# Transposing the modulation rows in 32x32 blocks on VectorE, and putting them into columns by four matmuls per layer

## The chip, the cores and the metric

The kernel runs on one core of a Trainium2 chip. The metric is the device time of one execution in microseconds (us). A core has five engines that run side by side, each through its own list of instructions in order, and they meet only at semaphores: TensorE (PE; its weight loads are listed apart as PEld), VectorE (DVE), ScalarE (ACT), GpSimd (POOL) and SyncE (SP), which here issues the weight transfers. TensorE reads SBUF and writes PSUM, which has eight banks of 128 x 512 fp32.

## The reference, cut to what matters

Two transformer-like blocks follow each other on 256 tokens of width 1024. The first has two layers (attention, cross attention to a memory, a gated feed-forward with a convolution of width 3 over tokens); the second has two layers whose inputs are modulated:

```python
def conv_glu(x, w_in, conv_w, conv_b, w_out):          # feed-forward, layers 0 and 1 of block one
    gate, val = jnp.split(x @ w_in, 2, axis=-1)        # (256, 1024) @ (1024, 5632)
    gate = depthwise conv of width 3 over tokens (gate) + conv_b
    return (jax.nn.gelu(gate, approximate=False) * val) @ w_out

def ada_params(sc, w, b):                              # block two; sc (n, D), w (D, 6 D)
    mod = sc @ w + b
    return [t[:, None, :] for t in jnp.split(mod, 6, axis=-1)]
```

`sc` is silu of the conditioning vector, once for the context and once for the latent tokens, so `sc @ w` is a product of 2 rows with a 1024 x 6144 matrix, for each of the two layers of block two.

## The kernel before, in words

Large matrices come in slabs of 1 MB (128 partitions x 2048 fp32). SP transfers them one after the other into a ring of four slots; a slot is refilled when PE has begun far enough ahead (`slab_begun`). Large products run in three passes for precision: ScalarE rounds a slab to `w_hi` (two instructions of 128x1024, L2497, function `hi`), GpSimd subtracts it from the slab to get `w_lo` (two of 128x1024, L1990, function `lo`), and PE adds `w_hi x_hi + w_lo x_hi + w_hi x_lo` (L1510 to L1514). PE may start a slab only when both halves of its `w_lo` are there (`lo_ready`).

The change sits in the two feed-forwards of block one, stages `f0` and `f1` (function `network` of each engine). There are 22 units of work, 20 in a loop of five rounds of four (`L.rounds(5, ...)`), two behind it. Between their slabs lie the 24 slabs of `ada_w`: block two's modulation of layer 0 is computed during `f0`, that of layer 1 during `f1`, since those matmuls need the slab only in its plain fp32 form. For unit n the engines do, each in this order:

- PE: `ada` (L1719): 8 matmuls of the modulation slab n, four of them side by side in the four groups of 32 partitions (quadrants) of bank 5 or 6, in turn; so the sum over the contraction is spread over the four quadrants, each with the 2 rows that are wanted. Then `col_T_split`: 48 matmuls of the weights of unit n into bank n mod 4. Then `ada_T` (L1736): two matmuls with the copied rows `modR` as the stationary operand and `pick` as the moving one (L1744). `pick` has two columns with ones where a partition is row 0 or 1 of its quadrant; so each adds the four quadrants and turns the two rows into two columns of bank 4. `ada_T` comes behind the copy `ada_out` of the same unit.
- ACT (L2542 to L2592): `ada_out`, a copy of bank 5 or 6 to `modR` (128x256, L2548, by way of L2435); the copy of bank n mod 4 to `raw` (128x512, also L2435); `hi` of unit n+2; a wait for `pre_ready` from DVE; the gelu (L2574).
- DVE (`gated`, L2145): waits for `raw`; the convolution (L2155, L2157, L2159; the last announces `pre_ready`); waits for the gelu; product with `val` (L2164); split into `h_hi` and `h_lo` (L2165, L2166).
- POOL: `lo` of unit n+2, two instructions, each waiting for its half from ACT.

Behind the 22 units PE does the last two modulation slabs (22 and 23) and their `ada_T`; then comes stage `fo0` or `fo1` (`rows_split`, L1549), 11 slabs with 24 matmuls each (L1564), each slab again behind `hi` and `lo`. DVE adds the bias to the 96 columns of bank 4 (`modulation`, L380, L384) behind its 22 units. In layer 1 more hangs on that: DVE goes on with `gains` and the variance of the context rows (L483, L528), POOL computes the power for it (`rstd(second=True)`) ahead of `lo` of slab 3 of `fo1` (L2060), and PE transposes the context rows ahead of slab 4 (`turn_ctx`, L1703).

Of the kernel before, what the change touches and what calls it, by code (L numbers as in the profile page):

```python
# [30 lines left out]
P = 128  # L31
# [78 lines left out]
for _name, _n in [("lambda", 256), ("subln", 128), ("dt_bias", 64), ("a_log", 64), ("d_skip", 32)]:  # L110
# [7 lines left out]
             "sq_ready", "wdt_hi", "wdt_ready", "c_split", "pre0_ready", "dt_ready", "yz_ready",  # L118
             "y_hi", "o_hi", "var_o", "rstd_o", "x_hi", "res_ready"]

# [55 lines left out]
def build(nc, slabs, x_in, xT_in, memT_in, ctx_in, pt_in, row_in, ln_in, wdt_in, out):  # L176
    with ExitStack() as ctx:
# [66 lines left out]
        half16 = small[:, 136:152]  # L244
        pick = small[:, 152:154]
        modA = small[:, 168:184]
# [34 lines left out]

        modR = cut(15360, 4, 256)
        raw = cut(11264, 4, 512)
# [1144 lines left out]
        def _(pe):  # L1428
# [3 lines left out]
            def free_of(b):  # L1432

                return free[last.get(b, "act")][b]
# [312 lines left out]

            def network(layer):
# [5 lines left out]
                for_rounds("act")  # L1754
                marks[stage] = {q: L.now(("act", q)) for q in range(8)}
                turned = turned_x()
                pe.wait_ge(free_of(4), frees(4))
                for b_ in (5, 6):
                    pe.wait_ge(free_of(b_), frees(b_))
                    last[b_] = "act"  # L1760
                per = {("act", q): 2 if q > 4 else 1 for q in (0, 1, 2, 3, 5, 6)}
                with L.rounds(5, per | {("took", "lo_ready"): 8}) as i:
                    for u in range(4):

                        ada(stage, 2 * u, u, 2 * i)
                        col_T_split(stage, 2 * u + 1, u, waits=turned if u == 0 else None)
                        ada_T(i * 4 + u, u)
                for u in range(2):
                    ada(stage, 2 * u, u, 10)
                    col_T_split(stage, 2 * u + 41, u)  # L1770
                    ada_T(20 + u, u)
# [297 lines left out]
        def _(v):  # L2069
# [75 lines left out]
            def gated(i, u, conv):  # L2145
# [78 lines left out]
            def network(stage, conv=None):  # L2224
# [6 lines left out]
                if conv is not None:  # L2231
                    one |= {("own", "v_step"): 4, ("own", "pre_ready"): 1}
                per = {k: 4 * n for k, n in one.items()} | {("raw", b): 1 for b in range(4)}
                with L.rounds(5, per) as i:
                    for u in range(4):
                        gated(i, u, conv)
                for u in range(2):
                    gated(5, u, conv)

            split_x("dq", by_chunks)  # L2240
# [23 lines left out]
            for tt in range(NT):  # L2264
# [7 lines left out]
                for g in (1, 2):  # L2272
# [18 lines left out]
            v.wait_ge(S["consts"], L.took("consts"))  # L2291
            v.tensor_reduce(pick, ident.rearrange("p (q c) -> p c q", q=4)[:, 0:2, :], AX.X,
                            ALU.add).then_inc(S["pick_ready"], 1)
# [135 lines left out]
        def _(a):  # L2429
# [112 lines left out]
            def network(func, conv, layer):  # L2542

                net, out_ = (f"f{layer}", f"fo{layer}") if conv else (f"h{layer}", f"ho{layer}")

                def ada_out(u):

                    copy_out(5 + u % 2, modR[:, u, :], bank[5 + u % 2][:, 0:256])  # L2548

# [9 lines left out]
                def one(i, u):  # L2559
                    if conv:  # L2560
                        ada_out(u)
                    else:
# [13 lines left out]
                if conv:  # L2576
                    per |= {("took", "pre_ready"): 4} | {(k, b): 2 for k in ("bank", "freed") for b in (5, 6)}
                if conv:
                    hi(net, 3)
                with L.rounds(5, per) as i:  # L2580
# [4 lines left out]
                if conv:  # L2585
                    for u in (2, 3):
                        ada_out(u)
                for j in range(1 if conv else 2, 11):
# [196 lines left out]
```

## Time and profile before

| | us |
|---|---|
| time, median of 3 runs (lowest to highest) | 2195.94 (2191.88 to 2202.35) |
| time of the profiled execution | 2195.72 |
| its span, first to last instruction | 2194.0 |
| PE busy | 2012.7 (92%) |
| POOL busy | 1255.3 (57%) |
| DVE busy | 1163.3 (53%) |
| ACT busy | 983.6 (45%) |
| stage f0 with the modulation of layer 0 | 306.1 to 484.6 |
| stage f1 with the modulation of layer 1 | 960.9 to 1141.2 |

A profile row names the line of the kernel, the engine, the operation, what it writes and reads with shapes, and its time. Brackets behind a row of a timeline give the idle time of the engine just before it and what ended that. Most buffers of the network are cut from one tensor, so `raw`, `pre`, `act` and `modR` all read `arena` in the rows. An fp32 matmul shows as two records (x192 for 96 instructions).

### The profile page before, as it was taken

What the parts mean: (1) busy time and instruction counts of PE and PEld (TensorE: products, weight loads), DVE (VectorE), ACT (ScalarE), POOL (GpSimd) and SP (SyncE); (2) the same over time, 40 slices, a digit from 0 to 9 for tenths busy, and PEclk for the clock granted to TensorE, in tenths of its full rate; (3) what the DMA queues carried; (4) which work ended last, traced back from release to release, by engine and by line L of the source; (5) the groups of instructions that cost most, each with busy time, mean ns of one, the idle gap of its engine ahead of it and who ended that gap; (6) DMA issues with size and microseconds to landing.
All of it is one profiled execution on the core that took longest, in us unless ns stands there. A gap on an engine that the chain in (4) does not pass through costs nothing.

```text
span 2194.0 us, 34395 instructions
## 1 busy us (share of the span) xinstructions
PE 2012.7 (92%) x13901; PEld 1792.8 (82%) x13901; DVE 1163.3 (53%) x1567; ACT 983.6 (45%) x1545; POOL 1255.3 (57%) x579
## 2 busy tenths in 40 slices
PE   7879999999899979979999899899999997978997
PEld 7768888878899966868888778788779986947996
DVE  8783247771200083157775655678846852745641
ACT  4454444543344373434453454444436645424542
POOL 8647566668688604546669334200087895415885
PEclk9989999999899999999999999999999998988999
DMA  6324366665455404366764222211144553313553
GB/s 246 132 97 175 114 245 266 270 234 181 167 191 191 175 1 154 116 235 254 276 247 176 73 77 94 80 58 58 39 154 154 191 191 116 135 58 137 186 185 115
DMA packets 48320, 342.30 MB, mean 156 GB/s; under 512 B 5264, under 2 KB 6288, under 8 KB 7248
## 3 DMA queue, kind: packets, MB, share of 16 engines
q1 hardware_dynamic: 45968, 328.22, 41.0%
q0 software_dynamic: 2240, 12.49, 1.5%
q8 instruction: 81, 1.33, 0.2%
q14 instruction: 31, 0.25, 0.0%
HBM read 339.65 MB, written 1.05 MB: 155 GB/s over the span
## 4 chain that ended last, share of the span: by engine, by line
PE 67%; DVE 20%; ACT 4%; DMA 3%; issue 3%; POOL 2%; DVEq 0%; SPq 0%; ACTq 0%; POOLq 0%
PE bank L1564 12%; PE bank L1510 9%; PE bank L1514 9%; PE bank L1512 9%; DMA ring<-slabs_dram 3%; PE bank L1484 3%; DVE arena L811 2%; PE bank L1608 2%; PE bank L1146 2%; PE bank L1149 2%; PE bank L1148 2%; PE bank L1545 2%; PE bank L1544 2%; PE bank L1542 2%; PE bank L1316 2%
## 5 line engine op out<-in xcount | busy, mean ns | idle before, releaser
L1990 POOL TENSOR_TENSOR w_lo<-ring,w_hi 128x1024 fp32r<-128x1024 f32 x360 | 877.6, 2463 | 333.2 <-ACT w_hi L2497 333.0
L1510 PE MATMUL bank<-x_hi,w_hi 128*128 128x256 f32 x2176 | 620.5, 285 | 27.8 <-POOL w_lo L1990 16.3
L1514 PE MATMUL bank<-x_lo,w_hi 128*128 128x256 f32 x2176 | 622.8, 286 | 0.0
L2497 ACT ACTIVATE w_hi<-ring 128x1024 fp32r<-128x1024 f32 x448 | 448.6, 1052 | 279.4 <-DMA ring<-slabs_dram 279.2
L1510 PEld LDWEIGHTS bank<-x_hi,w_hi 128*128 128x128 f32 x2176 | 419.2, 193 | 48.8 <-issue 44.7
L1514 PEld LDWEIGHTS bank<-x_lo,w_hi 128*128 128x128 f32 x2176 | 418.0, 192 | 0.0
L1512 PE MATMUL bank<-x_hi,w_lo 128*128 128x256 f32 x1472 | 414.2, 281 | 0.0
L2435 ACT ACTIVATE arena<-bank 128x512 f32<-128x512 f32 (+1 forms) x274 | 146.3, 548 | 349.4 <-PE bank L1514 242.1
L1990 POOL TENSOR_TENSOR w_hi<-ring,w_hi 128x1024 fp32r<-128x1024 f32 x88 | 217.7, 2496 | 130.8 <-ACT w_hi L2497 130.8
L1512 PEld LDWEIGHTS bank<-x_hi,w_lo 128*128 128x128 f32 x1472 | 282.5, 192 | 0.0
L1512 PE MATMUL bank<-x_hi,w_hi 128*128 128x256 f32 x704 | 201.5, 286 | 0.0
L2164 DVE TENSOR_TENSOR arena<-arena 128x256 f32<-128x256 f32 x88 | 112.7, 1281 | 110.0 <-ACT arena L2574 107.2
L403 POOL TENSOR_TENSOR w_lo<-ring,w_swo 128x1024 fp32r<-128x1024 f32 x16 | 39.9, 2526 | 185.0 <-ACT w_swo L911 185.0
L394 POOL TENSOR_TENSOR w_lo<-ring,w_half 128x1024 fp32r<-128x1024 f32 x32 | 76.9, 2409 | 113.8 <-ACT w_half L902 113.8
L1512 PEld LDWEIGHTS bank<-x_hi,w_hi 128*128 128x128 f32 x704 | 136.6, 194 | 0.0
L2395 DVE CUSTOM_DVE_ANT_0 arena<-bank,dist 128x512 f32<-128x512 f32 x32 | 22.1, 692 | 213.2 <-PE bank L1882 212.6
L2166 DVE TENSOR_TENSOR h_lo<-arena,h_hi 128x256 f32 (+1 forms) x88 | 118.5, 1347 | 10.1
L634 DVE SCALAR_TENSOR_TENSOR arena<-bank,pt,arena 128x508 f32<-128x508 f32 (+3 forms) x128 | 87.3, 682 | 62.6 <-ACT arena L917 59.0
L1564 PE MATMUL bank<-w_hi,h_hi 128*128 128x512 f32 x352 | 112.9, 398 | 2.1 <-issue 1.6
L1564 PE MATMUL bank<-w_lo,h_hi 128*128 128x512 f32 x352 | 112.8, 398 | 0.0
L1564 PE MATMUL bank<-w_hi,h_lo 128*128 128x512 f32 x352 | 112.5, 397 | 0.0
L1146 PE MATMUL bank<-s_hi,w_half 128*128 128x512 f32 (+1 forms) x288 | 103.9, 361 | 1.9 <-DVE s_lo L572 1.9
(323 smaller groups left out, 3808.2 us busy)
## 6 DMA issues: line engine op xcount, KB each, us to landing
ring<-slabs_dram SPq DMA_DIRECT2D x312, 1024.0 KB, 4.8
lnrow<-ln_dram POOLq DMA_DIRECT2D x6, 1024.0 KB, 5.1
xt<-xT_dram SPq DMA_DIRECT2D x1, 1024.0 KB, 5.7
xt<-memT_dram POOLq DMA_DIRECT2D x1, 1024.0 KB, 13.3
x<-x_dram POOLq DMA_DIRECT2D x1, 1024.0 KB, 17.2
arena<-ctx_dram POOLq DMA_DIRECT2D x1, 1024.0 KB, 8.2
lnrow<-ln_dram POOLq DMA_DIRECT2D x2, 512.0 KB, 4.0
res<-x POOLq DMA_DIRECT2D x2, 512.0 KB, 2.9
```

Of the source, the lines that this page charges most:

```text
L394: pool.tensor_tensor(half_slab(w_lo, c), half_slab(ring, c), half_of(c)[:, :, :].bitcast(F32), ALU.subtract).then_inc(S["lo_ready"], 1)
L634: ins = v.scalar_tensor_tensor(out=d3[:, :, lo:hi], in0=s3[:, :, lo + o:hi + o], scalar=pt[:, scw + k * 32 + j:scw + k * 32 + j + 1], in1= ...
L1146: ins = pe.matmul(dst, wh[:, k, :], hi_(k), start=(k == 0), stop=False)
L1510: ins = pe.matmul(dst, wh[:, k, c], src[0][:, k, :], start=(k == 0), stop=False)
L1512: ins = pe.matmul(dst, wl[:, k, c], src[0][:, k, :], start=False, stop=False)
L1514: ins = pe.matmul(dst, wh[:, k, c], src[1][:, k, :], start=False, stop=(k == KC - 1))
L1564: ins = pe.matmul(bank[2 * tt + h][:, :], st, w[:, k, h * 512:(h + 1) * 512], start=(first and n == 0), stop=(end and n == 2))
L1990: pool.tensor_tensor(dst[:, c], ring[:, s, c], w_hi[:, s, c].bitcast(F32), ALU.subtract).then_inc(S["lo_ready"], 1)
L2164: step(v.tensor_tensor(act[:, u, :], act[:, u, :], val, ALU.mult))
L2166: v.tensor_tensor(h_lo[:, j, :], act[:, u, :], h_hi[:, j, :].bitcast(F32), ALU.subtract).then_inc(S["hT_ready"], 1)
L2435: a.activation(dst, bank[b][:, :] if src is None else src, ACT.Copy if not kw else ACT.Identity, **kw).then_inc(free["act"][b], 1)
L2497: a.activation(w_hi[:, g % RING, c], ring[:, g % RING, c], ACT.Copy) \
```

## The change

`modR` is no longer copied by ScalarE and turned by PE for each slab. VectorE reads bank 5 or 6 and transposes it in 32x32 blocks into `modR` (two buffers now, `turn_ada`), as the first thing of each unit; ScalarE then copies 16 of the 256 columns (two of each block of 32) to a buffer `modC` that keeps all 24 slabs (`ada_out`). `ada_T` goes. In its place `ada_columns` runs once per layer, ahead of slab 2 of `fo0` and `fo1`: four matmuls, one for each quadrant, with `pick` (now 32 columns) as the stationary operand. Bank 4 has the same 96 columns in the end.

```diff
@@ tensor engine @@
-                fill(ins, b, "act")
-
-            def ada_T(j, r):
-                pe.wait_ge(free_of(5 + r % 2), frees(5 + r % 2))
-                for ch in range(2):
-                    at = 2 * (2 * j + ch)
-                    dst = bank[4][:, at:at + 2] if isinstance(j, int) \
-                        else bank[4][:, 0:96][:, bass.ds(at, 2)]
-                    ins = pe.matmul(dst, modR[:, r, ch * P:(ch + 1) * P], pick, start=True,
-                                    stop=True)
-                return ins
+                fill(ins, b, "dve")
+
+            def ada_columns(layer):
+                pe.wait_ge(free_of(4), frees(4))
+                pe.wait_ge(S["ada_kept"], 24 * (layer + 1))
+                kept = modC.rearrange("p u (c q s) -> p q (u c) s", c=2, q=4)
+                for q in range(4):
+                    ins = pe.matmul(bank[4][32 * q:32 * (q + 1), 0:96].rearrange("p (a s) -> p a s", s=2),
+                                    pick, kept[:, q, :, :], start=True, stop=True)
+                fill(ins, 4, "dve")
...
                         col_T_split(stage, 2 * u + 1, u, waits=turned if u == 0 else None)
-                        ada_T(i * 4 + u, u)
...
-                ada_T(22, 2)
-                fill(ada_T(23, 3), 4, "dve")
-                rows_split(f"fo{layer}", hook=turn_ctx if layer else None)
+                def between(j):
+                    if j == 2:
+                        ada_columns(layer)
+                    if layer:
+                        turn_ctx(j)
+                rows_split(f"fo{layer}", hook=between)
@@ vector engine @@
+            def turn_ada(u):
+                b = 5 + u % 2
+                v.wait_ge(full["dve"][b], L.filled(b))
+                v.transpose(modR[:, u % 2, :], bank[b][:, 0:256]).then_inc(free["dve"][b], 1)
+                v.wait_ge(free["dve"][b], L.freed(b))
...
                     for u in range(4):
+                        if conv is not None:
+                            turn_ada(u)
                         gated(i, u, conv)
                 for u in range(2):
+                    if conv is not None:
+                        turn_ada(u)
                     gated(5, u, conv)
+                if conv is not None:
+                    turn_ada(2)
+                    turn_ada(3)
@@ scalar engine @@
-                def ada_out(u):
-                    copy_out(5 + u % 2, modR[:, u, :], bank[5 + u % 2][:, 0:256])
+                def ada_out(u, j):
+                    b = 5 + u % 2
+                    a.wait_ge(free["dve"][b], L.up(("turned", b)))
+                    a.activation(modC[:, j, :].rearrange("p (c s) -> p c s", s=2),
+                                 modR[:, u % 2, :].rearrange("p (c s) -> p c s", s=32)[:, :, 0:2],
+                                 ACT.Copy).then_inc(S["ada_kept"], 1)
```

## Rows read from the trace of the kernel before

**Rows 1.** Stretch f0: busy PE, PEld, DVE, ACT, POOL; clock, DMA share, GB/s.

```profile
306.10:484.60 178.50, 167.01 (x1537) 151.04 (x1537) 129.06 (x130) 86.11 (x124) 109.32 (x45) 0.98 0.70 271
```

**Rows 2.** Timeline of PE in f0: an unhindered step, then a stalled one.

```profile
391.97 0.50 PE L1744 MATMUL bank<-small,arena 128*128 128x2 f32 x4
392.40 1.07 PE L1730 MATMUL bank<-ring,sc_in 128*32 128x256 f32 x16
...
415.64 0.60 PE L1744 MATMUL bank<-small,arena 128*128 128x2 f32 x4 [1.93 <-ACT arena L2435]
```

**Rows 3.** Waits: PE's before L1744, both layers; DVE's for raw in f0.

```profile
  ACT arena L2435: 21.1, 13
...
DVE arena L2155 <- ACT arena L2435: 27.5, 4, 21.4
```

**Rows 4.** Timelines of DVE, ACT and POOL, 346.8 to 356.1: unit 4 of f0.

```profile
347.70 0.41 DVE L2155 TENSOR_SCALAR arena<-arena,pt 128x256 f32<-128x256 f32 x1 [1.39 <-ACT arena L2435]
...
348.89 2.40 DVE L2159 SCALAR_TENSOR_TENSOR arena<-arena,pt 128x255 f32<-128x255 f32 x1
351.84 1.98 DVE L2164 TENSOR_TENSOR arena<-arena 128x256 f32<-128x256 f32 x1 [0.56 <-ACT arena L2574]
...
354.38 0.42 DVE L2166 TENSOR_TENSOR h_lo<-arena,h_hi 128x256 f32 x1
...
346.84 0.60 ACT L2435 ACTIVATE arena<-bank 128x512 f32<-128x512 f32 x1 [1.90 <-PE bank L1514]
347.33 2.00 ACT L2497 ACTIVATE w_hi<-ring 128x1024 fp32r<-128x1024 f32 x2
...
351.32 0.42 ACT L2574 ACTIVATE arena<-arena 128x256 f32<-128x256 f32 x1 [0.68 <-DVE arena L2159]
...
348.46 5.08 POOL L1990 TENSOR_TENSOR w_hi<-ring,w_hi 128x1024 fp32r<-128x1024 f32 x2 [3.41 <-ACT w_hi L2497]
```

**Rows 5.** Timeline of DVE, 399 to 410: a cast beside POOL; the loop's return.

```profile
405.44 2.26 DVE L2165 CAST h_hi<-arena 128x256 f32 x1
...
408.98 0.42 DVE L2155 TENSOR_SCALAR arena<-arena,pt 128x256 f32<-128x256 f32 x1 [0.73 <-DVE h_lo L2166]
```

**Rows 6.** DVE reading PSUM (a timeline row); ACT's small copy (groups by form).

```profile
870.10 2.87 DVE L2207 TENSOR_TENSOR x_lo<-bank,x_hi 128x512 fp32r<-128x512 f32 x4 [5.00 <-ACT x_hi L2468]
...
L2609 ACT ACTIVATE sc_in<-pt 128x16 f32<-128x16 f32 x1 | 0.2, 218 | 0.0
```

**Rows 7.** Timeline of DVE: the first product of f0 and of f1.

```profile
319.64 2.34 DVE L2164 TENSOR_TENSOR arena<-arena 128x256 f32<-128x256 f32 x1 [2.81 <-ACT arena L2574]
...
976.78 2.31 DVE L2164 TENSOR_TENSOR arena<-arena 128x256 f32<-128x256 f32 x1 [4.73 <-ACT arena L2574]
```

**Rows 8.** Timelines of DVE, ACT, POOL, PE at f0's end; last row: the chain.

```profile
474.17 0.42 DVE L2166 TENSOR_TENSOR h_lo<-arena,h_hi 128x256 fp32r<-128x256 f32 x1
...
482.73 1.94 DVE L2164 TENSOR_TENSOR arena<-arena 128x256 f32<-128x256 f32 x1 [0.55 <-ACT arena L2574]
...
489.63 0.26 DVE L384 TENSOR_TENSOR mod<-bank,pt 128x96 f32<-128x96 f32 x1
...
470.74 0.60 ACT L2435 ACTIVATE arena<-bank 128x512 f32<-128x512 f32 x1 [1.31 <-PE bank L1514]
...
477.93 0.60 ACT L2435 ACTIVATE arena<-bank 128x512 f32<-128x512 f32 x1 [4.38 <-PE bank L1514]
...
479.55 14.69 POOL L1990 TENSOR_TENSOR w_lo<-ring,w_hi 128x1024 fp32r<-128x1024 f32 x6 [11.76 <-ACT w_hi L2497]
...
482.96 1.67 PE L1744 MATMUL bank<-small,arena 128*128 128x2 f32 x8 [2.86 <-ACT arena L2435]
...
484.62 57.93 PE bank L1564 x239
```

**Rows 9.** Timelines at f1's end: ACT's last copy of raw, POOL's power.

```profile
1134.54 0.60 ACT L2435 ACTIVATE arena<-bank 128x512 f32<-128x512 f32 x1 [2.85 <-PE bank L1514]
...
1151.07 0.71 POOL L1967 TENSOR_TENSOR small<-small 128x2 f32<-128x2 f32 x1
```

More of the change, by code:

```diff
@@ L118 @@
              "sq_ready", "wdt_hi", "wdt_ready", "c_split", "pre0_ready", "dt_ready", "yz_ready",
-             "y_hi", "o_hi", "var_o", "rstd_o", "x_hi", "res_ready"]
+             "y_hi", "o_hi", "var_o", "rstd_o", "x_hi", "res_ready", "ada_kept"]
 class Ledger:
@@ L244, in build @@
         half16 = small[:, 136:152]
-        pick = small[:, 152:154]
+        pick = small[:, 264:296]
         modA = small[:, 168:184]
@@ L280, in build @@
         goT = tri[:, :, :, :].rearrange("p a b c -> p (a b c)").rearrange("p (a b) -> p a b", a=8)
-        modR = cut(15360, 4, 256)
+        modR = cut(15360, 2, 256)
+        modC = cut(15872, 24, 16)
         raw = cut(11264, 4, 512)
@@ L1755, in network @@
                 marks[stage] = {q: L.now(("act", q)) for q in range(8)}
+                marks[f"ada{layer}"] = {b: L.now(("dve", b)) for b in (5, 6)}
                 turned = turned_x()
-                pe.wait_ge(free_of(4), frees(4))
                 for b_ in (5, 6):
                     pe.wait_ge(free_of(b_), frees(b_))
-                    last[b_] = "act"
-                per = {("act", q): 2 if q > 4 else 1 for q in (0, 1, 2, 3, 5, 6)}
+                    last[b_] = "dve"
+                per = {("act", q): 1 for q in range(4)} | {("dve", q): 2 for q in (5, 6)}
                 with L.rounds(5, per | {("took", "lo_ready"): 8}) as i:
@@ L1770, in network @@
                     col_T_split(stage, 2 * u + 41, u)
-                    ada_T(20 + u, u)
                 ada(stage, 4, 2, 10)
                 ada(stage, 5, 3, 10, last_one=True)
-                ada_T(22, 2)
-                fill(ada_T(23, 3), 4, "dve")
-                rows_split(f"fo{layer}", hook=turn_ctx if layer else None)
+                def between(j):
[4 more added lines that the diff above has]
+                rows_split(f"fo{layer}", hook=between)
             pe.wait_ge(S["consts"], L.took("consts"))
@@ L2233, in network @@
                 per = {k: 4 * n for k, n in one.items()} | {("raw", b): 1 for b in range(4)}
+                if conv is not None:
+                    per |= {(k, b): 2 for k in ("bank", "freed") for b in (5, 6)}
                 with L.rounds(5, per) as i:
                     for u in range(4):
+                        if conv is not None:
+                            turn_ada(u)
                         gated(i, u, conv)
                 for u in range(2):
+                    if conv is not None:
+                        turn_ada(u)
                     gated(5, u, conv)
+                if conv is not None:
+                    turn_ada(2)
+                    turn_ada(3)
             split_x("dq", by_chunks)
@@ L2291, in _ @@
             v.wait_ge(S["consts"], L.took("consts"))
-            v.tensor_reduce(pick, ident.rearrange("p (q c) -> p c q", q=4)[:, 0:2, :], AX.X,
+            v.tensor_reduce(pick, ident.rearrange("p (q c) -> p c q", q=4), AX.X,
                             ALU.add).then_inc(S["pick_ready"], 1)
@@ L2560, in one @@
                     if conv:
-                        ada_out(u)
+                        ada_out(u, i * 4 + u)
                     else:
@@ L2576, in network @@
                 if conv:
-                    per |= {("took", "pre_ready"): 4} | {(k, b): 2 for k in ("bank", "freed") for b in (5, 6)}
+                    per |= {("took", "pre_ready"): 4, ("turned", 5): 2, ("turned", 6): 2}
                 if conv:
+                    L.n.update({("turned", b): marks[f"ada{layer}"][b] for b in (5, 6)})
                     hi(net, 3)
@@ L2586, in network @@
                     for u in (2, 3):
-                        ada_out(u)
+                        ada_out(u, 20 + u)
                 for j in range(1 if conv else 2, 11):
```

## The prediction

> **What bounds the kernel now.** PE is busy for 92% of the whole, so the first guess is that whatever leaves PE is won. I read the two stages that the change touches by themselves, and there it is not so. The busy time by stretch gives PE 167.0 of 178.5 us in f0, DVE 129.1, POOL 109.3, ACT 86.1 [rows 1]; nobody looks full but PE. Next the timeline of PE. An unhindered step has its last `ada_T` at 391.97 and the next `ada` at 392.40, so `ada_T` holds PE for 0.43 us of a step; a stalled one stood idle for 1.93 us before `ada_T`, for the copy on ACT [rows 2]. These stalls come to 21.1 us over both layers, in 13 places [rows 3]. A copy of 0.4 us doesn't make a PE wait for 1.9: ACT does it late, since in its list it stands behind the gelu of the unit before, and the gelu behind DVE's convolution. So DVE is asked next.
>
> Rows 4 show one unit on the three engines. The copy of `raw` ends at 347.44 (346.84 + 0.60), DVE starts 0.26 later, its third instruction (L2159) takes 2.40 us, the gelu ends at 351.74, the product takes 1.98, and DVE is done at 354.80. The same instructions take 0.48 and 0.43 us when POOL is still. POOL's two subtractions run from 348.46 to 353.54: L2159 ends 0.3 us behind POOL's first, L2164 0.3 behind its second. A cast beside POOL's work took 2.26 us in the same way [rows 5]. So DVE stands still for most of POOL's 5 us in each unit. DVE waited for `raw` in only four of f0's 22 units, and 21.4 of those 27.5 us are before the first [rows 3]: its 129 us of work [rows 1], with the gelu and the semaphores between, fill the stage. In f0 and f1 DVE and POOL set the pace together with PE, with nothing to spare. That is where the change puts more work.
>
> **The change part by part.** *Removed from PE:* 22 `ada_T` in the loop at 0.43 us and the waits before them. By itself that is 2 x 22 x 0.43 = 19 us and up to 21.1 us, if PE still sets the pace; it is idle time gained if not.
>
> *The order that is new.* Before, ACT could copy `raw` of unit n+1 as soon as PE had filled the bank and the gelu of unit n was done, while DVE was still busy with the product and the split of unit n. Now the copy of `raw` stands in ACT's list behind `ada_out`, which waits for `turn_ada` of the same unit, and that stands in DVE's list behind the split of unit n. Behind the waiting ACT instruction are queued: the copy of `raw`, `hi` for unit n+2 and so POOL's `lo` for it, and the gelu. So a closed ring arises: DVE's split, transpose, small copy, copy of `raw`, `hi`, POOL's two subtractions (which hold up DVE), DVE's product, split. I walk it once.
>
> - From the end of a `raw` copy to the end of the split: 354.80 - 347.44 = 7.36 us [rows 4]. This row is the right one since there `hi` followed the copy at once (347.33), as it will: the slab is asked for when PE begins unit n, and by then ACT is late.
> - The transpose. No row shows one. It reads 256 columns of PSUM. Of DVE instructions that read PSUM the one of 512 columns takes 2.87/4 = 0.72 us [rows 6] and the one of 96 columns 0.26 [rows 8]: 1.1 ns a column, so 0.43 us. Bounds: 0.26 (the smallest row) and 0.86 (twice the rate's price, should 4-byte blocks go at half speed); I take 0.43, and 0.14 us for the semaphore before it. Beside POOL it may stand or not: a cast from SBUF does (2.26), the PSUM row L384 was done in 0.26 us at 489.63, inside POOL's 479.55 to 494.24 [rows 8]. In this ring it comes 1.4 us behind POOL's end, so it is not hit.
> - ACT's copy of 16 columns: 0.22 us, the row of that size [rows 6], and 0.03 before it. Bounds 0.15 and 0.4.
> - The copy of `raw`, 0.60, less 0.1 that ACT overlaps (the next one started at 347.33, before 347.44): 0.5.
>
> Together 7.36 + 0.57 + 0.25 + 0.50 = 8.68 us a unit. At the loop's return DVE stands 0.73 us before its first instruction [rows 5], of which some 0.28 are there in any unit (0.26 in [rows 4]): 0.45 more in each fourth unit, now inside the ring.
>
> The Trainium skill has two prices for the transpose. VectorE: DVE Perf Modes, section on the TRN2 errata, gives a PSUM to SBUF instruction 120 cycles and one for each element at 0.96 GHz, an estimate of 0.39 us; its section on the three transpose paths has 0.311 us for 128x128 in bf16, to which 128 more columns at the trace's 1.1 ns would add up to 0.45. By the one the sum would be 2 us less, by the other 1 us more; no run here shows it yet.
>
> *f0.* The first unit is untouched up to the product, since DVE has nothing before it. That starts at 319.64 and takes 2.34 [rows 7]; cast and split end 1.0 later, at 322.96; then transpose, small copy and copy of `raw` (1.32): the `raw` copy of unit 1 ends at 324.3. Units 1 to 19 are followed by POOL's work of unit n+2 (`hi` runs up to unit 21): 324.3 + 18 x 8.68 + 4 x 0.45 = 482.3 for unit 19, 491.5 for unit 20 with the last return. Unit 20 has no POOL work beside it: in the rows its `raw` copy ended at 471.34 and its split at 474.59, so 3.25, and 1.2 for the new steps: `raw` of unit 21 is copied at 496.0. Before it was at 478.53 [rows 8]. PE is no limit: `lo` of unit 21 is ready 6.1 us behind `raw` of 19 (353.54 - 347.44), so at 488.4, its matmuls last about 5.8 (a step of 7.2 less `ada` and `ada_T`), so 494.2. The stage is late by 17.5 us.
>
> *The end of f0.* PE starts fo0 when POOL has `lo` of its slab 0: 484.62, 6.1 us behind the last `raw` [rows 8], before as after; the 2.86 us that PE waited in the last `ada_T` [rows 8] lay under this wait, so nothing is won. But ACT's `hi` of slab 1 now stands behind the small copies of slabs 22 and 23, and these behind DVE's two last transposes. DVE's product ends at 484.67 [rows 8], 6.1 behind `raw`; POOL is idle then, so cast, split and two transposes take 0.3 + 0.4 + 0.9, the last small copy 0.25: `hi` starts at 8.0, its first half takes 1.0, POOL 4.9 for its two (14.69/3): slab 1 is ready 13.9 to 14.0 us behind `raw`. PE is done with slab 0 at 6.1 + 5.3 (58/11) = 11.4. It waits 2.5 us. From then on POOL's 4.9 a slab is under PE's 5.3. The four matmuls, 8 records of 96 columns, are bounded by the 1.07 us of 16 records of 256 columns at L1730 [rows 2] from above and by 8/16 x 96/256 of it, 0.2, from below; I take 0.5 us a layer. In f0 the sum is 17.5 + 2.5 + 0.5 = 20.5 us.
>
> *f1.* The product of the first unit starts at 976.78, 2.31 [rows 7]: `raw` of unit 1 at 981.4, of unit 21 at 1153.1, against 1135.14 [rows 9]: 18.0 late. The same 2.5 and 0.5. Then one new wait: POOL's power (0.71 [rows 9]) stands ahead of `lo` of slab 3 and hangs on DVE's `modulation`, which now waits for `ada_columns` ahead of slab 2. From the matmuls' end: DVE's 0.26, two small instructions 0.4, power 0.71, slab 3's `lo` 4.9, with semaphores 6.4, while PE has slab 2's 5.3: 1.1 us of stall. Behind the waiting POOL are slabs 3 to 10, behind the waiting DVE the context rows, which PE wants only ahead of slab 4: 5 us to spare. Sum 18.0 + 2.5 + 0.5 + 1.1 = 22.1.
>
> **Sum.** 20.5 + 22.1 = 42.6 us on the profiled execution's 2195.72 (span 2194.0), which is within 0.3 us of the median 2195.94: 2238.3.
>
> **The rivals.**
>
> *Unchanged ring (same).* POOL's subtractions could shift so that the new steps lie under them: two of DVE's instructions are held for 2 us each, and if a transpose and a `raw` copy ran in those 4 us, the unit would stay at its present mean, 178.5/22 = 8.1 with all stalls. Then only the ends are lost, 3.0 + 4.1: 2203. Against it: POOL cannot start until ACT's `hi`, and that is behind the very copy. From none to all hidden the loop gives 0 to 36 us.
>
> *PE sets the pace (faster).* If the ring closes in less than 7.19 - 0.43 = 6.76 us, PE is the bound and gains 19 us of `ada_T` and its stalls, 21.1 less 2 x 2.9 that lay under POOL at the two ends [rows 8]: 2195.7 - 34 = 2161. For it: the 21.1 us are real and their cause goes. Against: DVE alone needs 7.3 in [rows 4]. It decides from a ring under 6.76.
>
> *A dear transpose (slower still).* At 0.86 us, 48 x 0.43 = 21 us more at most, of which 44 lie in the ring: 19, so 2257. It decides from the first microsecond, since nothing in the ring covers it.
>
> *The transposes alone (slower, smaller).* ACT's order doesn't bite, as where PE or the DMA is late anyway, and only DVE's 0.57 us a unit are added, 44 x 0.57 = 25; the places where DVE waited for `raw` behind the first unit, 6.1 us in f0 [rows 3] and taken twice, swallow 12, and the ends cost 7: 2195.7 + 25 - 12 + 7 = 2216. Against it: the copy order is in the lists, whoever else is late.
>
> **How the numbers follow.** The forecast, 2238.3 with 2227 to 2249 of its own, 0.50; dear transpose 0.13; transposes alone 0.17; unchanged 0.12; faster 0.08. The range reaches from 2211 to 2259: it leaves out the last two, 0.20 together. Half a per cent is 11 us, about what a measurement of this kernel can tell from no change: faster 0.08, same 0.12, slower 0.80.
>
> **What would show it.** In the profile after: a line `modR`'s transpose of about 0.43 us, 24 a layer; the `raw` copies on ACT released no longer by PE but following DVE; steps of 8.7 us and PE idle some 2 us before each unit's first matmul, released by POOL's `w_lo`; f0 about 196 us long and f1 about 198; a gap of 2.5 us behind the first 24 matmuls of fo0. It is wrong if the steps stay at 8.1 (the ring hides), if they fall to 6.8 (PE's pace), or if PE's waits are named for bank 5 or 6 instead of `w_lo`. The granted clock, 0.98 in f0 now [rows 1], should not matter, as PE has 2 us to spare in each step.

## The result, and the profile after

| | before | after |
|---|---|---|
| time, median (lowest to highest), us | 2197.62 (2191.88 to 2202.35) | 2245.36 (2240.49 to 2247.87) |
| profiled execution, us (span) | 2195.72 (2194.0) | 2240.49 (2238.8) |
| stage f0, us | 178.4 | 200.3 |
| fo0, to the first sum that DVE takes from it | 58.1 | 58.6 |
| stage f1, us | 180.4 | 203.2 |
| fo1, to the first sum that DVE takes from it | 58.9 | 62.7 |

The kernel is slower: the ratio is 1.0216, with a 95% interval of 1.0184 to 1.0247. The profiled executions differ by 44.8 us, of which the two stages have 21.9 and 22.8, fo0 0.5 and fo1 3.8; the rest of the kernel was 4.2 shorter, 3.4 of them ahead of f0, where only `pick` was made wider. That part isn't the change's: in the profiled runs below that have the same lists up to f0 as the kernel after, f0 begins anywhere from 301.4 to 306.4 us.

First the busy time of the engines over the whole, then of PE, PEld, DVE, ACT and POOL in f0 and f1 (the last three columns are the granted clock, the DMA share and GB/s).

```profile
PE 2003.7 (89%) x13725; PEld 1779.0 (79%) x13725; DVE 1181.7 (53%) x1615; ACT 974.0 (44%) x1545; POOL 1258.5 (56%) x579
...
302.70:503.00 200.30, 163.25 (x1441) 145.81 (x1441) 136.37 (x152) 79.51 (x120) 109.19 (x44) 0.94 0.62 241
979.33:1182.50 203.17, 165.22 (x1440) 147.08 (x1441) 135.28 (x153) 78.55 (x120) 109.50 (x44) 0.93 0.62 243
```

Against [rows 1], PE's work in f0 fell by 3.8 us and the stage grew by 21.9; every engine has more idle time than before. No engine is full, so I looked for a circle of waits. One unit shows it, on the timelines of DVE, ACT, POOL and PE of the kernel after (start, duration, engine, line; in brackets the idle time before and what ended it):

```profile
331.21 2.39 DVE L2161 SCALAR_TENSOR_TENSOR arena<-arena,pt 128x255 f32<-128x255 f32 x1
334.16 1.94 DVE L2166 TENSOR_TENSOR arena<-arena 128x256 f32<-128x256 f32 x1 [0.55 <-ACT arena L2596]
...
336.79 0.43 DVE L2168 TENSOR_TENSOR h_lo<-arena,h_hi 128x256 f32 x1 [0.26 <-DVE h_hi L2167]
337.25 0.45 DVE L2176 STREAM_TRANSPOSE arena<-bank 128x256 f32<-128x256 f32 x1
338.73 0.41 DVE L2157 TENSOR_SCALAR arena<-arena,pt 128x256 f32<-128x256 f32 x1 [1.03 <-ACT arena L2453]
...
337.83 0.22 ACT L2568 ACTIVATE arena<-arena 128x16 f32 x1 [3.78 <-DVE arena L2176]
337.96 0.58 ACT L2453 ACTIVATE arena<-bank 128x512 f32<-128x512 f32 x1
338.44 1.99 ACT L2515 ACTIVATE w_hi<-ring 128x1024 fp32r<-128x1024 f32 x2
...
339.56 4.98 POOL L1992 TENSOR_TENSOR w_hi<-ring,w_hi 128x1024 fp32r<-128x1024 f32 x2 [3.75 <-ACT w_hi L2515]
...
336.16 0.36 PE L1511 MATMUL bank<-x_hi,w_hi 128*128 128x256 f32 x1 [1.89 <-POOL w_hi L1992]
```

Read it as a circle: DVE's split (336.79), the transpose (337.25 to 337.70), the small copy (337.83), the copy of `raw` (337.96 to 338.54), `hi`, POOL (from 339.56), which holds up one convolution and the product of the next unit (2.39 and 1.94 here), and so the next split. ACT is idle 3.78 us before the small copy, for DVE's transpose. In [rows 4] it was idle 1.90 us before its copy of `raw`, and for PE. PE now waits for POOL. Where the profile names no releaser ("issue") it can be the same wait: PE's 1.64 us of that name before 489.87 ended 0.1 us behind POOL's pair for that unit (484.82 + 4.95 = 489.77). The waits of the kernel after (us in total, times, longest) and two groups of instructions (busy us, mean ns of one | idle time before them):

```profile
PE bank L1511 <- POOL w_hi L1992: 33.0, 20, 3.7
PE bank L1511 <- issue: 31.2, 15, 3.5
...
DVE arena L2157 <- ACT arena L2453: 67.8, 44, 7.0
...
L2176 DVE STREAM_TRANSPOSE arena<-bank 128x256 f32<-128x256 f32 x48 | 21.6, 450 | 24.9 <-PE bank L1731 18.0 <-DVE h_lo L2168 4.7
...
L2568 ACT ACT_TABLE_LOAD x10 | 12.8, 1283 | 34.9 <-DVE arena L2176 34.9
```

DVE waited for `raw` in 4 of f0's 22 units before [rows 3]; now it waits in all 44 of both stages.

### The profile page after: what moved, and what is told of

It reads as the page before. It is cut to its first block, busy times and chain, and to the rows that moved or that the text cites. A ratio compares the mean times of both kernels' runs of the same rounds, so it can differ in the third digit from the quotient of the medians.

```text
span 2238.8 us, 34066 instructions
## 1 busy us (share of the span) xinstructions
PE 2003.7 (89%) x13725; PEld 1779.0 (79%) x13725; DVE 1181.7 (53%) x1615; ACT 974.0 (44%) x1545; POOL 1258.5 (56%) x579
## 3 DMA queue, kind: packets, MB, share of 16 engines
HBM read 339.65 MB, written 1.05 MB: 152 GB/s over the span
## 4 chain that ended last, share of the span: by engine, by line
PE 59%; DVE 25%; ACT 6%; issue 4%; POOL 3%; DMA 2%; DVEq 1%; ACTq 0%; SPq 0%; POOLq 0%
PE bank L1565 11%; PE bank L1515 8%; PE bank L1511 8%; PE bank L1513 7%; DVE arena L2161 4%; DVE arena L2166 4%; PE bank L1485 3%; POOL w_lo L1992 2%; DMA ring<-slabs_dram 2%; DVE arena L812 2%; PE bank L1609 2%; PE bank L1147 2%; PE bank L1149 2%; PE bank L1150 2%; PE bank L1546 2%
## 5 line engine op out<-in xcount | busy, mean ns | idle before, releaser
L1511 PE MATMUL bank<-x_hi,w_hi 128*128 128x256 f32 x2176 | 625.8, 288 | 92.2 <-POOL w_hi L1992 33.0
L1511 PEld LDWEIGHTS bank<-x_hi,w_hi 128*128 128x128 f32 x2176 | 424.3, 195 | 113.9 <-issue 109.1
L1515 PEld LDWEIGHTS bank<-x_lo,w_hi 128*128 128x128 f32 x2176 | 423.3, 195 | 0.0
L2453 ACT ACTIVATE arena<-bank 128x512 f32<-128x512 f32 (+1 forms) x226 | 129.1, 582 | 287.9 <-PE bank L1515 185.0
L1513 PE MATMUL bank<-x_hi,w_hi 128*128 128x256 f32 x704 | 206.8, 294 | 0.0
L2166 DVE TENSOR_TENSOR arena<-arena 128x256 f32<-128x256 f32 x88 | 134.0, 1523 | 98.7 <-ACT arena L2596 96.3
L1513 PEld LDWEIGHTS bank<-x_hi,w_hi 128*128 128x128 f32 x704 | 143.0, 203 | 0.0
L635 DVE SCALAR_TENSOR_TENSOR arena<-bank,pt,arena 128x508 f32<-128x508 f32 (+3 forms) x128 | 87.2, 682 | 62.6 <-ACT arena L918 59.0
```

The source lines that it names most:

```text
L635: ins = v.scalar_tensor_tensor(out=d3[:, :, lo:hi], in0=s3[:, :, lo + o:hi + o], scalar=pt[:, scw + k * 32 + j:scw + k * 32 + j + 1], in1= ...
L1511: ins = pe.matmul(dst, wh[:, k, c], src[0][:, k, :], start=(k == 0), stop=False)
L1513: ins = pe.matmul(dst, wl[:, k, c], src[0][:, k, :], start=False, stop=False)
L1515: ins = pe.matmul(dst, wh[:, k, c], src[1][:, k, :], start=False, stop=(k == KC - 1))
L2166: step(v.tensor_tensor(act[:, u, :], act[:, u, :], val, ALU.mult))
L2453: a.activation(dst, bank[b][:, :] if src is None else src, ACT.Copy if not kw else ACT.Identity, **kw).then_inc(free["act"][b], 1)
```

## Experiments

The theory is that the order of ACT's list closes the ring: ACT reaches the copy of `raw` only behind DVE's split and transpose. The rivals are that DVE's own added work costs the time wherever it stands, and that PE was the bound all along and something else stalls it. Each run is set against the kernel before, timed beside it. "Step" is the time between the ends of two copies of `raw` on ACT in f0, read from its timeline. Where "the four stages" are named, they are f0, fo0, f1 and fo1 of the profiled execution; a table of them stands at the end of this section. A PE that nothing hinders sets the step to 7.19 us before and to 6.85 without `ada_T`.

**The order on ACT.** The small copy moves behind the copy of `raw` and `hi`; DVE is left as it is.

```diff
                 def one(i, u):
-                    if conv:
-                        ada_out(u, i * 4 + u)
-                    else:
+                    if not conv:
                         ahead(4 * i + u) if isinstance(i, int) else ahead(u, i)
...
                         ahead(4 * i + u) if isinstance(i, int) else ahead(u, i)
+                        ada_out(u, i * 4 + u)
                         a.wait_ge(S["pre_ready"], L.took("pre_ready"))
```

> The changed kernel with only ScalarE's list reordered in the two stages: copy of raw, hi of unit n+2, then the small copy of the transposed block, then the gelu. The transposes stay first in VectorE's unit. Theory (the closed ring made by the order in ScalarE's list is the cost): the ring of 8.7 us opens, the copy of raw follows PE again, steps fall to the 7.8 us of before plus about 0.5 us for the transpose on VectorE where it isn't covered; the time comes to 2205 to 2218 us, 27 to 40 us under the changed kernel. Rival (the transposes alone, wherever the copies stand, or PE's own waits cost the time): 2240 or more, steps stay near 8.7 us.

Measured: 2205.08 us, ratio 1.004 (1.0024 to 1.0056), at the lower edge of what was expected. Of the change's 48 us this one move gives back 40. Outside the loop's returns the step falls from 8.66 us (mean) to some 7.65 (7.26 to 7.70 behind the first three). f0 and f1 are as long as in the kernel before: 177.9 and 181.2 us against 178.4 and 180.4. So nearly all that the change costs in these two stages is the order; what DVE's added work costs and PE's lost work brings cancel in sum. Of the 9.1 us by which this span is still longer than that of the kernel before, 5.3 lie in fo0 and fo1 (there PE waited 1.7 us for `w_lo` behind slab 0 of each, the stall that the prediction had for the kernel after, and 1.2 us ahead of slab 3 of fo1), and 3.5 outside the four stages. What sets the step now is seen at the loop's return, on the timelines of DVE and ACT of this kernel:

```profile
345.07 0.45 DVE L2176 STREAM_TRANSPOSE arena<-bank 128x256 f32<-128x256 f32 x1 [0.59 <-DVE h_lo L2168]
345.88 2.57 DVE L2157 TENSOR_SCALAR arena<-arena,pt 128x256 f32<-128x256 f32 x1 [0.35 <-DVE arena L2176]
348.59 2.33 DVE L2159 SCALAR_TENSOR_TENSOR arena<-arena,pt 128x255 f32<-128x255 f32 x1
...
342.99 1.28 ACT L2453 ACT_TABLE_LOAD   x1
344.28 0.60 ACT L2453 ACTIVATE arena<-bank 128x512 f32<-128x512 f32 x1
```

`raw` lies ready from 344.88 and DVE comes to it at 345.88: here DVE itself is what is late, with two instructions held by POOL one behind the other. The run doesn't tell apart whether the small copy had to go behind the copy of `raw` only or behind `hi` too.

**The transpose in DVE's gap.** DVE stands idle about 0.55 us for each gelu. The transpose is put there, and the small copy behind the gelu on ACT; the last transpose waits for the small copy before it, since the two share a buffer.

```diff
                     v.wait_ge(S["pre_ready"], L.own("pre_ready"))
+                    turn_ada(u)
                 v.wait_ge(S["act_ready"], L.took("act_ready"))
...
-                        if conv is not None:
-                            turn_ada(u)
                         gated(i, u, conv)
...
                     turn_ada(2)
+                    v.wait_ge(S["ada_kept"], 24 * conv + 22)
                     turn_ada(3)
...
                     a.activation(act[:, u, :], src, func).then_inc(S["act_ready"], 1)
+                    if conv:
+                        ada_out(u, i * 4 + u)
```

> As the run with raw first, and besides the transpose of a unit is moved behind the convolution, into the 0.55 us in which VectorE waits for the gelu, and the small copy behind the gelu. Theory: the transpose of 0.45 us is covered, VectorE's unit is as long as before the change, PE has 0.43 us less a step; 2190 to 2203 us, about the kernel before. What could take it back: bank 5 or 6 is freed later, so PE may wait before a modulation slab. Rival (the 48 transposes cost by themselves): at least 22 us more than that, 2218 or more.

Measured: 2201.58 us, 1.0021 (1.0002 to 1.0039). It is 3.5 us less than the run before it, not the 20 us that 44 transposes last. A wait took the gap's place; here PE's waits in this kernel, and a stretch of DVE's and PE's timelines:

```profile
PE bank L1731 <- DVE arena L2177: 39.5, 29, 3.9
...
387.10 0.45 DVE L2177 STREAM_TRANSPOSE arena<-bank 128x256 f32<-128x256 f32 x1
...
387.69 1.07 PE L1731 MATMUL bank<-ring,sc_in 128*32 128x256 f32 x16 [1.42 <-DVE arena L2177]
```

The transpose frees bank 5 or 6, and it now comes late in DVE's unit. PE wants the bank back two units on and meets the wait ahead of its modulation slab.

**More banks for it.** The modulation takes banks 4 to 7 in turn (bank 4 is not needed until `ada_columns`), and the two last small copies go behind `hi` of slab 1 of fo0 and fo1.

```diff
-                b = 5 + r % 2
+                b = 4 + r % 4
...
                     hi(out_, j)
+                    if conv and j == 1:
+                        for u in (2, 3):
+                            ada_out(u, 20 + u)
```

> As the kernel with the transpose in the gelu's gap, with the modulation slabs in four banks (4 to 7) in turn instead of two (5, 6), and the small copies of slabs 22 and 23 behind hi of slab 1 of the next stage. In the run before PE waited 39.5 us for the transpose to free its bank. Theory (VectorE with GpSimd beside it sets the pace at 7.7 us, PE's wait for the bank only hands that on): PE's wait moves to w_lo, the time falls little, 2188 to 2200. Rival (the bank's wait cost the time): 15 us or more go, 2185 or less.

Measured: 2194.72 us, 1.0004 (0.9988 to 1.002): the whole loss of the change is gone, and nothing is won on the kernel before. The wait for L2177 is gone from PE's list; POOL's `w_lo` stands in its place with 14.4 us in 8 places, and "issue" with 14.9 in 14. By stages it is no standstill: f0 and f1 are 3.4 us shorter than in the kernel before (177.4 and 178.0), and fo1 is 3.7 longer (62.6), as in the kernel after; the wait ahead of its slab 3 is again 1.17 us.

**The table load at the loop's return.** One step in four after was 10.4 us long, not 8.66. Timelines of DVE and ACT at such a return in the kernel after:

```profile
345.38 0.42 DVE L2168 TENSOR_TENSOR h_lo<-arena,h_hi 128x256 f32 x1
346.39 0.45 DVE L2176 STREAM_TRANSPOSE arena<-bank 128x256 f32<-128x256 f32 x1 [0.59 <-DVE h_lo L2168]
349.24 0.41 DVE L2157 TENSOR_SCALAR arena<-arena,pt 128x256 f32<-128x256 f32 x1 [2.39 <-ACT arena L2453]
...
346.98 1.28 ACT L2568 ACT_TABLE_LOAD   x1 [4.23 <-DVE arena L2176]
348.27 0.22 ACT L2568 ACTIVATE arena<-arena 128x16 f32 x1
348.39 0.58 ACT L2453 ACTIVATE arena<-bank 128x512 f32<-128x512 f32 x1
```

ACT loads a table for its first copy of each round, 1.28 us, and the load stands behind the wait for the transpose though ACT had been idle for 4.23 us. (The round's other load, for the gelu, begins at 350.89 ahead of the gelu's wait for DVE, which lasts 0.65 us longer than the load; it costs nothing.) The experiment gives ACT a one-element copy ahead of that wait, so that the load comes early.

```diff
                 with L.rounds(5, per) as i:
+                    if conv:
+                        a.activation(small[:, 297:298], pt[:, 0:1], ACT.Copy)
                     for u in range(4):
```

> The changed kernel with one more ScalarE instruction at the head of each loop round, a copy of one column that waits for nothing. The activation table that is loaded at the head of each round then comes before the wait for the transpose. Theory (the round's table load of 1.28 us stands inside the ring, a term that the prediction had at nothing): 4 to 5 loads a layer leave the ring, 10 to 13 us less than the changed kernel, 2232 to 2236. Rival (that load lies beside other work): no change, 2245.

Measured: 2237.81 us, 1.019 (1.0158 to 1.0222), 1.8 us above what was expected. The four returns of f0 fell from 10.36 to 10.43 us to 9.07 to 9.16, 1.28 us each. ACT's timeline in this kernel:

```profile
346.40 1.28 ACT L2605 ACT_TABLE_LOAD   x1
347.70 0.20 ACT L2605 ACTIVATE small<-pt 128x1 f32<-128x1 f32 x1
350.63 0.22 ACT L2568 ACTIVATE arena<-arena 128x16 f32 x1 [2.73 <-DVE arena L2176]
```

The load has ended 2.9 us before the transpose is done. Eight returns at 1.28 are 10 us, and the four stages are 10.7 us shorter than in the kernel after; the medians of the runs differ by 7.6, and the intervals of the two ratios overlap, so the steps carry this finding and the time only agrees with it.

**What the removal is worth alone.** The kernel before without the 22 `ada_T` of each loop.

```diff
                         col_T_split(stage, 2 * u + 1, u, waits=turned if u == 0 else None)
-                        ada_T(i * 4 + u, u)
...
                     col_T_split(stage, 2 * u + 41, u)
-                    ada_T(20 + u, u)
```

> The kernel before without the two matmuls per modulation slab on PE for slabs 0 to 21 (the modulation columns are left wrong, only those of slabs 22 and 23 are made); the copies on ScalarE stay. It measures what the removal on PE is worth by itself. Theory (VectorE and GpSimd set the pace of the stages): little, 0 to 10 us less than before, 2187 to 2197. Rival (PE sets the pace): 19 us of matmuls and some 15 us of waits go, 2162.

Measured: 2193.89 us, 0.9986 (0.9968 to 1.0003). PE lost 14.5 us of work and 14.7 of the 21.1 us of named stalls (the two ahead of the last `ada_T` of each stage stay, 6.4 us), and the time hardly moved. PE's waits in this kernel show what stayed and the places that took over:

```profile
PE bank L1510 <- POOL w_hi L1988: 13.7, 8, 2.8
PE bank L1510 <- issue: 13.1, 11, 2.7
PE bank L1744 <- ACT arena L2433: 6.4, 2, 3.2
```

Neither of the first two was on PE's list before but for 0.7 us of "issue". So the rival that PE sets the pace falls: by the interval this part of the change could bring 0.3% at most.

**What one transpose costs.** The kernel after, with each transpose done twice into the same place.

```diff
+                step(v.transpose(modR[:, u % 2, :], bank[b][:, 0:256]))
                 v.transpose(modR[:, u % 2, :], bank[b][:, 0:256]).then_inc(free["dve"][b], 1)
```

> The changed kernel with each of the 48 transposes done twice, one after the other. Theory (nothing in the ring covers VectorE's transpose, its 0.45 us counts in full): 0.45 us and 0.1 us for the semaphore in some 42 units of both layers, 23 us more, 2265 to 2271, steps of 9.25 us. Rival (the transpose lies beside other work and only the order costs): 2245 to 2250.

Measured: 2267.62 us, 1.0343 (1.0325 to 1.0361), which is 22.3 us over the kernel after (the four stages: 21.5), or 0.46 us for each of the 48, the full duration (449 ns) and a little between the two. Nothing covers any of it: the transpose stands in the ring. The steps rose from between 8.57 and 8.77 us to between 9.04 and 9.24.

**What POOL's hold on DVE is worth.** The kernel after, with POOL's subtractions over half of the columns in f0 and f1.

```diff
                     c = slice(h * SLAB // 2, (h + 1) * SLAB // 2)
+                    if stage in ("f0", "f1"):
+                        c = slice(h * SLAB // 2, h * SLAB // 2 + SLAB // 4)
```

> The changed kernel with GpSimd's subtractions of the two stages over half the columns (128x512 instead of 128x1024; half of w_lo is left as it was, so the correction of half the contraction is wrong). Theory (GpSimd's 5 us hold VectorE up inside the ring): 2 x 1.2 us of each unit go, the ring would take 6.2 us, PE's 6.8 us take over, 7.9 at the loop's return: 2160 to 2172. Rival (GpSimd's work lies beside VectorE's and costs nothing): 2240 or more.

Measured: 2158.0 us, 0.9841 (0.9825 to 0.9857). DVE's and POOL's timelines in this kernel:

```profile
348.38 1.29 DVE L2163 SCALAR_TENSOR_TENSOR arena<-arena,pt 128x255 f32<-128x255 f32 x1
350.22 0.88 DVE L2168 TENSOR_TENSOR arena<-arena 128x256 f32<-128x256 f32 x1 [0.56 <-ACT arena L2598]
...
347.96 2.86 POOL L1994 TENSOR_TENSOR w_hi<-ring,w_hi 128x512 fp32r<-128x512 f32 x2 [3.61 <-ACT w_hi L2517]
```

POOL's pair takes 2.86 us in place of 4.98, and the step went from 8.66 to 6.5 (6.40 to 6.59): all of POOL's 2.1 us come out of the ring. The time is 2 us below what was expected. With the returns (8.17 to 8.32) the mean step of a round is 6.8 us and PE is busy for 152.8 of f0's 157.7, so it is PE that now sets the mean pace. The two DVE instructions lost 2.2 us, from 2.39 and 1.94 to 1.29 and 0.88.

**Work off DVE.** If DVE is the bound, moving one of its instructions to ACT must pay where removing work from PE didn't. The convolution's first instruction, a scale and a bias, is done by ACT from the bank, ahead of the copy of `raw`; first on top of the version with four banks, then on the kernel before by itself.

```diff
+                        a.activation(pre[:, u, :], bank[u][:, 0:T], ACT.Identity,
+                                     scale=col(PT[f"cw{layer}"].start + FC),
+                                     bias=col(PT[f"cb{layer}"].start)).then_inc(S["a_step"], 1)
                     copy_out(u, raw[:, u, :])
...
-                    step(v.tensor_scalar(p, gate, w(1), pt_col(PT[f"cb{conv}"].start, j), ALU.mult,
-                                         ALU.add))
```

> As the run with four banks, and the convolution's first instruction (scale and bias of the gate half, 128x256) moved from VectorE to ScalarE, which reads the bank itself. Theory (VectorE's list sets the pace): 0.41 us and its semaphore go from each unit, 0.55 x 44 = 24 us less at most, partly taken by PE's 6.8 us a step and by ScalarE's 0.5 us more: 2168 to 2188, below both kernels. Rival (VectorE isn't the bound once the order is mended): within 5 us of the four-bank run.

> The kernel before, with its turning on PE, and only the convolution's first instruction moved from VectorE to ScalarE. It asks whether the transposes on VectorE had any part in the gain of the run with that move. Theory (with VectorE 0.55 us shorter a unit, the stage comes near PE's step, 7.2 us with the turning and 6.8 without): the same move gains here too, but some 5 to 10 us less of it: 2177 to 2187. Rival (the transposes are worth nothing anywhere): 2175, the same as the run with both.

> The run with the transpose in the gap, four banks and the first instruction on ScalarE once more, beside the one above on the same chip: 2172 to 2178, in both theories.

Measured: with the transposes 2174.94 us, 0.9925 (0.9901 to 0.9948), and again 2175.11, 0.9901 (0.9875 to 0.9928); on the kernel before 2183.74, 0.9931 (0.9906 to 0.9956). Both beat the kernel before. PE's waits in the kernel before with the move show where that came from:

```profile
PE bank L1744 <- ACT arena L2433: 6.4, 6, 1.4
```

The 21.1 us of [rows 3] are down to 6.4, and 19 of its 21 steps in f0 lie between 7.05 and 7.90 us, most of them within 0.1 of PE's 7.19. f0 and f1 together are 19 us shorter than in the kernel before (168.8 and 170.9). With `ada_T` gone as well the mean step is 7.21 against 7.31 there. The medians of the two versions timed together differ by 8.6 us, but their intervals overlap between 0.9906 and 0.9928, and the four stages of the profiled executions differ by 1.1 us only: f0 and f1 are 3.2 us shorter with the transposes, fo1 is 2.3 longer. That the transposes add something on top isn't shown.

**Where the time lies.** The stages of every profiled execution, in us; "rest" is its span less the four stages.

| kernel | f0 | fo0 | f1 | fo1 | sum | rest |
|---|---|---|---|---|---|---|
| before | 178.4 | 58.1 | 180.4 | 58.9 | 475.8 | 1718.2 |
| after | 200.3 | 58.6 | 203.2 | 62.7 | 524.8 | 1714.0 |
| after, `raw` first on ACT | 177.9 | 59.6 | 181.2 | 62.7 | 481.4 | 1721.7 |
| and the transpose in the gap | 178.6 | 58.5 | 180.2 | 61.6 | 478.9 | 1717.0 |
| and four banks | 177.4 | 57.7 | 178.0 | 62.6 | 475.7 | 1717.2 |
| and the move to ACT | 166.9 | 57.7 | 169.4 | 61.0 | 455.0 | 1718.7 |
| the same again | 167.4 | 58.0 | 169.1 | 61.1 | 455.6 | 1717.2 |
| before, the move to ACT | 168.8 | 58.2 | 170.9 | 58.8 | 456.7 | 1730.2 |
| before, less `ada_T` | 177.0 | 57.4 | 178.4 | 60.1 | 472.9 | 1719.5 |
| after, table early | 195.3 | 58.8 | 198.2 | 61.8 | 514.1 | 1721.6 |
| after, transposes twice | 210.0 | 59.6 | 214.0 | 62.7 | 546.3 | 1716.9 |
| after, half of `lo` | 157.7 | 58.6 | 151.8 | 62.7 | 430.9 | 1723.5 |

The rest, where nothing of note was changed, differs by up to 16 us from one execution to another. So for differences of a few us the stages say more than the whole.

## Why the prediction was right

2238.3 was forecast and 2245.4 measured, inside the range of 2211 to 2259 and its own 2227 to 2249. The mechanism is the one that was forecast. That the sum was 42.6 us for the profiled execution's 44.8 is closer than its terms deserve: in the four stages themselves the loss was 49.0 us. The loop's returns were 10 us short of that and two stalls of 2.5 us didn't come, and 4.2 us of variation elsewhere did the rest.

- **The bound.** DVE and POOL with PE, and not PE alone: confirmed by three runs: work off PE gave 0.9986 of the kernel before, work off DVE 0.9931, and less of POOL's took the kernel after from 1.0216 to 0.9841. One term was mis-sized: `ada_T` holds PE for 0.34 us of a step (7.19 - 6.85, and 14.5 us of PE's work for the 44), not 0.43, so PE's pace lay at 6.85 and not 6.76.
- **The ring.** Predicted 8.68 us a unit; the 14 steps of f0 that are neither first, return, nor exit run from 8.57 to 8.77, mean 8.66. Its terms: the transpose 0.43 for 0.45 measured, the small copy 0.22 for 0.218, the copy of `raw` as before. Unit 1's `raw` was to end 18.2 us into the stage (324.3 - 306.1) and ended 18.4 us into it.
- **The loop's return, the step that was off.** It was priced at 0.45 us, now inside the ring; it cost 10.4 - 8.66 = 1.7. What was missing is the table load of 1.28 us that ACT does for its first copy of a round. Before, it lay in ACT's own slack, ahead of the copies; I left it out as if that slack were still there. ACT's timeline of the kernel before has it 2.3 us ahead of the copy of `raw` at 346.84, which then waited for PE [rows 4]:

```profile
343.26 1.28 ACT L2435 ACT_TABLE_LOAD   x1
```

  Four returns a layer make 5.1 us, two layers 10. Against that the exit into unit 20 was priced at 9.13 and took 8.63. Together: f0 late by 21.9 us (17.5 predicted), f1 by 22.8 (18.0).
- **The stall of 2.5 us in fo0 and fo1 did not come.** POOL was on time to the tenth: slab 1's `w_lo` was to be ready 13.9 to 14.0 us behind the last `raw` (497.00), so at 511.0. The step that failed is the length of PE's slab 0, taken as the mean 5.3 of eleven slabs. (That mean was itself misread: the row of 57.93 us in [rows 8] has 239 matmuls, which are ten slabs of 24; a plain slab takes 5.55 us.) Timelines of PE and POOL of the kernel after:

```profile
502.99 1.19 PE L1565 MATMUL bank<-w_hi,h_hi 128*128 128x512 f32 x2 [5.37 <-POOL w_lo L1992]
...
511.07 0.70 PE L1565 MATMUL bank<-w_hi,h_hi 128*128 128x512 f32 x2
...
516.79 0.38 PE L1744 MATMUL bank<-arena,small 128*32 128x96 f32 x8
...
506.16 14.22 POOL L1992 TENSOR_TENSOR w_lo<-ring,w_hi 128x1024 fp32r<-128x1024 f32 x6 [3.32 <-ACT w_hi L2515]
```

  Slab 0 lasted 8.1 us (502.99 to 511.07) and slab 1 5.7. The first matmuls take 1.05 us a pair, later ones 0.62. The windows below give the clock: 0.50, which is 1.2 GHz, for the first 5 us, behind an idle stretch of 5.37 us; in the kernel before it was the same at this place, where the trace that I had when I took 5.3 already showed it, and slab 0 lasted 8.15 us there too. First the kernel after, all engines:

```profile
502.90:507.90 5.00, 4.91 (x12) 3.89 (x13) 1.85 (x5) 3.20 (x6) 1.74 (x1) 0.50 0.58 206
```

  and the kernel before, PE at L1564 alone:

```profile
484.50:489.50 5.00, 4.96 (x12) 0.50 0.53 210
```

  The slow slab covers the late `w_lo`, so fo0 grew by the four matmuls alone: 0.38 us by the row at 516.79 where I took 0.5.
- **The granted clock.** That it "should not matter" held for the loop, where it fell from 0.98 to 0.94 in f0 while PE had time to spare, and not for the ends: it is the reason for the long slab 0 of fo0, and for 0.9 us more in fo1.
- **The wait through DVE and POOL in f1** came by the path worked out, 1.1 us of stall predicted and 1.17 measured. The size is in part luck: the chain from the four matmuls to slab 3 took 6.9 us where I had 6.4, and PE's slab 2 5.8 where I had 5.3. Timelines of POOL, PE and DVE of the kernel after, at the start of fo1:

```profile
1197.57 0.71 POOL L1969 TENSOR_TENSOR small<-small 128x2 f32<-128x2 f32 x1 [2.40 <-DVE small L529]
1198.26 29.75 POOL L1992 TENSOR_TENSOR w_lo<-ring,w_hi 128x1024 fp32r<-128x1024 f32 x12
...
1203.60 0.70 PE L1565 MATMUL bank<-w_hi,h_hi 128*128 128x512 f32 x2 [1.17 <-POOL w_lo L1992]
...
1219.14 9.15 DVE L552 CAST s_hi<-xt 128x512 fp32r<-128x512 f32 x1 [12.32 <-ACT xt L865]
```

  fo1 lost 3.8 us (4.1 predicted), but not from the terms that I had: 1.17 and 0.38 are as priced, 0.9 came from slab 0, which took 8.1 us here and 7.2 before, about 0.9 from DVE, which was held in the cast at 1219.14 and came late to the sums, and the other 0.4 from gaps of 0.1 us or so at the heads of slabs. The total is near by luck.
- **The rivals.** A hidden ring (2203) and PE's pace (2161) are out. "The transposes alone" put 25 us on DVE's work, less 12 that its waits swallow, and 7 on the ends. The run with ACT's order undone lost 0.3 us in f0 and f1, not 13, and 5.3 at the ends: with the ring open DVE's added work costs no more than what PE gains. Its 2205 lies by the 2203 of the hidden ring, for another reason: there the steps were to stay as before though the ring is closed. The dear transpose is out, at 0.45 us.

The Trainium skill had two prices for the transpose. VectorE: DVE Perf Modes gives by its errata table an estimate of 0.39 us and by its section on the three transpose paths one of 0.45; the 48 rows have a mean of 450 ns, so the second came nearer, though its 0.311 us is for bf16 and its slope is this trace's. The Trainium skill, SBUF — State Buffer, "Who interferes with whom", says that a VectorE instruction with at most one SBUF input, outside the two-port modes, doesn't contend with GpSimd. The version with four banks and the move to ACT shows such a case; DVE's and POOL's timelines:

```profile
386.61 0.45 DVE L2175 STREAM_TRANSPOSE arena<-bank 128x256 f32<-128x256 f32 x1
387.51 1.60 DVE L2165 TENSOR_TENSOR arena<-arena 128x256 f32<-128x256 f32 x1 [0.46 <-ACT arena L2598]
...
386.24 5.10 POOL L1992 TENSOR_TENSOR w_hi<-ring,w_hi 128x1024 fp32r<-128x1024 f32 x2 [3.31 <-ACT w_hi L2511]
```

Inside POOL's 5.10 us the transpose, which reads PSUM, takes its 0.45, and the product of two SBUF operands behind it is held to 1.60. The trace agrees with this rule.

## What to carry to other kernels

Before a wait for another engine is put at the head of an in-order list, write down all that stands behind it, table loads too, and follow it round: if the engine waited for depends on any of it, the waits add up to a ring, though no engine is full. Moving only one small copy on ACT behind the instructions that did not need it gave back 40 of 48 us. And a stall named on the busiest engine isn't its price: taking 29 us of work and stalls from PE gave 0.1%, while moving a 0.4 us instruction of each unit off DVE gave 0.7%.

## What the runs showed of the hardware

- A table load on ACT can stand behind a wait of the instruction that needs it, and does so here for the first copy of a round: 1.28 us behind 4.23 us of idle time. A one-element copy (128x1) ahead of the wait took it out of the path. It isn't always so: in the same round of the kernel after the gelu's load came ahead of the gelu's wait for DVE. What decides it is open.

```profile
350.89 1.28 ACT L2596 ACT_TABLE_LOAD   x1
352.82 0.42 ACT L2596 ACTIVATE arena<-arena 128x256 f32<-128x256 f32 x1 [0.65 <-DVE arena L2161]
```

- A DVE instruction can be held over several POOL instructions, not only one: the cast at 1219.14 took 9.15 us, until POOL's run of 12 subtractions of 2.5 us each ended at 1228.01; the same cast took 0.82 us before, and 2.5 us in its later calls.
- Behind 5.4 us without a matmul, PE had a granted clock of 0.50 for the first 5 us of fo0 and of fo1, and its matmuls took 1.05 us a pair for 0.62. In fo1 of the kernel before PE had stood idle for 2.95 us before its last `ada_T` and for 0.53 us before its first matmul, the granted clock was still 0.99 from 1141 to 1142 us and 0.50 from 1142 to 1145, and slab 0 took 7.2 us and not 8.1.
